# The merge stage of a hybrid decoder block: full products in blocks, or pairs of seven quarter products

## What is computed

```python
proj = rms_norm(h) @ w_in + b_in      # u, v, q, k, vg, r, g_lr, gate_a, gate_b
ya = chunked_sgu(gelu(u), gelu(v), ...)      # 512 x 1024
yb = gla(q, k, vg, gk, r, ...)               # 512 x 1024
merged = sigmoid(gate_a) * (ya @ w_branch_a) + sigmoid(gate_b) * (yb @ w_branch_b)
h = h + merged @ w_out
xn2 = rms_norm(h)
h = h + (silu(xn2 @ w_ffn_gate) * (xn2 @ w_ffn_up)) @ w_ffn_down
y = rms_norm(h)
```

## Time and profile before

| what | value |
|---|---|
| median of three executions | 844.11 us (842.53 to 844.25) |
| the profiled execution | 842.62 us |
| its span, first to last instruction | 840.8 us |
| PE busy | 829.6 us, 99% of the span |
| DVE, ACT, POOL busy | 420.9, 370.9, 342.3 us |
| matmuls of the merge stage | from 266.69 to 441.18 us |
| granted TensorE clock | 0.999 of full speed |

### The profile page before, as it was taken

The page is one execution under the profiler, slowest core; times in us unless marked ns, Lnnn a source line. Parts: engine busy times, 40 slices in busy tenths (PEclk is TensorE's granted clock), DMA queues, the critical chain, the costliest instruction groups (busy, mean ns, idle before and its releaser), DMA issues.

```text
span 840.8 us, 11971 instructions
## 1 busy us (share of the span) xinstructions
PE 829.6 (99%) x4720; PEld 727.9 (87%) x4720; DVE 420.9 (50%) x419; ACT 370.9 (44%) x393; POOL 342.3 (41%) x100
## 2 busy tenths in 40 slices
PE   8999999999999999999999999999999999999996
PEld 7888888788888888888888899999999999888885
DVE  5375337674665721221213269766666667244445
ACT  5522446665666523231312565545445555122233
POOL 4444433324224343434444432644444445544440
PEclk9999999999999999999999999999999999999999
DMA  8842222122112122222225133433333320322212
GB/s 334 287 174 83 86 83 101 51 100 94 49 57 100 51 101 100 100 100 100 98 101 186 65 101 101 128 109 112 109 124 110 106 100 30 138 80 88 93 47 101
DMA packets 17511, 89.88 MB, mean 107 GB/s; under 512 B 1744, under 2 KB 2000, under 8 KB 10704
## 3 DMA queue, kind: packets, MB, share of 16 engines
q1 hardware_dynamic: 15088, 81.83, 27.8%
q10 hardware_dynamic: 2400, 7.73, 2.8%
HBM read 87.46 MB, written 2.10 MB: 107 GB/s over the span
## 4 chain that ended last, share of the span: by engine, by line
PE 88%; DVE 5%; ACT 2%; issue 2%; DMA 2%; POOL 1%; DVEq 0%; SPq 0%; ACTq 0%; POOLq 0%
PE acc L1159 11%; PE acc L1160 11%; PE acc L1161 11%; PE acc L1178 9%; PE acc L1177 9%; PE acc L1176 9%; PE acc L1421 7%; PE acc L1424 7%; PE acc L1423 7%; PE acc L1202 3%; DMA wp<-wstream 1%; DVE vgs L842 1%; PE acc L1295 1%; PE acc L1333 1%; PE acc L1338 1%
## 5 line engine op out<-in xcount | busy, mean ns | idle before, releaser
L333 POOL TENSOR_TENSOR w_lo<-raw,w_hi 128x2048 fp32r<-128x2048 f32 x52 | 239.7, 4610 | 342.9 <-ACT w_hi L410 342.9
L410 ACT ACTIVATE w_hi<-raw 128x2048 fp32r<-128x2048 f32 x52 | 99.3, 1912 | 216.1 <-PE acc L1178 138.8
L1159 PE MATMUL acc<-xt_hi,w_hi 128*128 128x512 f32 (+1 forms) x368 | 140.3, 381 | 0.2 <-ACT yb L520 0.2
L1160 PE MATMUL acc<-xt_lo,w_hi 128*128 128x512 f32 (+1 forms) x368 | 138.1, 375 | 0.0
L1161 PE MATMUL acc<-xt_hi,w_lo 128*128 128x512 f32 (+1 forms) x368 | 138.1, 375 | 0.0
L357 POOL TENSOR_TENSOR A_lo<-wp,A_hi 128x1024 fp32r<-128x1024 f32 x30 | 72.3, 2409 | 97.5 <-ACT A_hi L618 97.5
L1159 PEld LDWEIGHTS acc<-xt_hi,w_hi 128*128 128x128 f32 x368 | 69.3, 188 | 13.9 <-issue 1.1
L1160 PEld LDWEIGHTS acc<-xt_lo,w_hi 128*128 128x128 f32 x368 | 69.3, 188 | 13.1 <-issue 0.9
L1161 PEld LDWEIGHTS acc<-xt_hi,w_lo 128*128 128x128 f32 x368 | 69.3, 188 | 12.4
L1074 DVE TENSOR_TENSOR al<-act,ah 128x1024 fp32r<-128x1024 f32 x11 | 48.2, 4382 | 63.0 <-ACT ah L671 63.0
L1176 PE MATMUL acc<-w_hi,ah 128*128 128x512 f32 x176 | 68.5, 389 | 0.0
(11 more groups left out here) (228 smaller groups left out, 1764.2 us busy)
## 6 DMA issues: line engine op xcount, KB each, us to landing
raw<-wstream SPq DMA_DIRECT2D x52, 1024.0 KB, 4.8
wp<-wstream SPq DMA_DIRECT2D x20, 1024.0 KB, 7.8
h<-x ACTq DMA_DIRECT2D x1, 2048.0 KB, 7.8
xw<-x_t SPq DMA_DIRECT2D x3, 512.0 KB, 9.5
out<-h SPq DMA_DIRECT2D x3, 512.0 KB, 2.6
xn_in<-x SPq DMA_DIRECT2D x2, 512.0 KB, 12.2
xn_in<-x ACTq DMA_DIRECT2D x2, 512.0 KB, 6.6
vbias_bc<-vbias ACTq DMA_DIRECT2D x1, 1024.0 KB, 9.6
```

The source lines that it names most:

```text
L333: pool.tensor_tensor(w_lo[s][:, :], raw[s][:, :], w_hi[s][:, :], ALU.subtract).then_inc(lo_ready, 1)
L410: a.activation(w_hi[s][:, :], raw[s][:, :], ACT.Copy).then_inc(hi_ready, 1)
L1159: pe.matmul(dst, wh[:, k, cs], rh[:, k, ts], start=(k == 0), stop=False)
L1160: pe.matmul(dst, wh[:, k, cs], rl[:, k, ts], start=False, stop=False)
```

## The change

Of the 16 merge blocks the first block of each gate (blocks 20 and 21) stay full products. The other 14 become seven pairs of the feed-forward kind: three pairs of gate blocks (moving operand `xt`), then two pairs with `ya` and two with `yb`. The stage's loops are written out.

- The sums t1 to t4 of `xt` are formed by DVE in the input stage, in the place of `xn_in`, sent by ACT to device memory (`turned_sums`, 4 x 512 KB) between two weight blocks, and brought back by SP before the merge stage.
- For `ya` and `yb` the sums are formed by DVE inside the pairs before (pairs 2, 3 and 4, 5), their high parts are taken by ACT and their low parts by DVE in pairs 3 and 5, and the plain quarters of `ya` and `yb` are written over `xt_hi` (ACT) and `xt_lo` (POOL, `refill`) between the products that still read the old content and those that read the new.
- The joined quarters (`mcq`) of a gate pair get their sigmoid by ACT (`gates_of`, four of 512 elements). Those of a branch pair are multiplied by the gates on POOL (`weighted`, two of 1024 elements). DVE adds the two branches in two halves (`merged_sum`), ACT and DVE split the sums (`merged_high`, `merged_low`).
- The first two output blocks are loaded to another place (`raw_out`), and their low parts are taken by POOL (`low_out`) in pair 7, ahead of `weighted(7)`.

The core of the diff:

```diff
+            v.wait_ge(xw_scaled, KD)
+            v.tensor_tensor(tx[0][:, :, :], x12, x11, ALU.subtract).then_inc(t_formed, 1)
+            v.tensor_tensor(tx[2][:, :, :], x22, x12, ALU.subtract).then_inc(t_formed, 1)
+            v.wait_ge(t_formed, 1)
+            v.tensor_tensor(tx[1][:, :, :], x22, tx[0][:, :, :], ALU.subtract).then_inc(t_formed, 1)
+            v.wait_ge(t_formed, 3)
+            v.tensor_tensor(tx[3][:, :, :], x21, tx[1][:, :, :], ALU.subtract).then_inc(t_formed, 1)
             v.wait_ge(xt_ready, 4)
             values(1)
...
-            for j in range(3):
+            high2(6, 0, block_used, 4)
+            a.wait_ge(t_formed, 4)
+            for n in range(4):
+                a.dma_start(turned_sums[n], tx[n][:, :, :].rearrange("p k t -> p (k t)")).then_inc(t_stored, 16)
+            for j in range(1, 3):
                 high2(6 + j, j % 2, block_used, 3 + j + 1)
...
+            def merge_pair(p):
+                c, nn = (p - 1) % 2, (p + 2) // 2 * 16
+                m = (p - 3) // 2
+                last = p == MERGE_PAIRS
+
+                if p > 1:
+                    form_s2(c)
+                    merge_c12(p - 1)
+                    s_low_of("S2", chain, 7 * p - 2)
+                    v.wait_ge(s_low, 4 * p - 1)
+                    form_s4(c)
+                if p in (4, 6):
+                    t_low_of((p - 4) // 2, 3)
+                if p in (2, 4):
+                    form_t12((p - 2) // 2)
+                if p in (3, 5):
+                    t_low_of(m, 0)
+                merge_u2(p)
+                if p == 1:
+                    merge_u3(p)
+                s_low_of("S4", chain, 7 * p)
+                if not last:
+                    v.wait_ge(s_low, 4 * p)
+                    form_s1(1 - c, nn, p + 1)
+                if p > 1:
+                    merge_u3(p)
+                merge_c22(p)
+                if not last:
+                    form_s3(1 - c)
+                if last:
+                    merged_sum(0)
+                if p in (2, 4):
+                    form_t3((p - 2) // 2)
+                if p in (3, 5):
+                    t_low_of(m, 1)
+                    t_low_of(m, 2)
+                    form_t4(m)
+                merge_c21(p)
+                if not last:
+                    s_low_of("S1", chain, 7 * p + 2)
+                    s_low_of("S3", diff, 7 * p + 3)
+                    v.wait_ge(s_low, 4 * p + 1)
+
+            for p in range(1, MERGE_PAIRS + 1):
+                merge_pair(p)
+            merged_low(0)
+            merge_c12(MERGE_PAIRS)
+            merged_sum(1)
+            merged_low(1)
...
+            def merge_pair(p):
+                c = (p - 1) % 2
+
+                a12_low(c, 7 * p + ((5 if p == 1 else 4) - 7))
+                if p > GATE_PAIRS + 1:
+                    weighted(p - 1)
+                a22_low(c, 7 * p - 1)
+                if p in (4, 6):
+                    refill(3 * ((p - 2) // 2), (ya, yb)[(p - 4) // 2], slice(4, 8), slice(HT, SEQ))
+                if p < MERGE_PAIRS:
+                    a11_low(1 - c, 7 * p + 1)
+                if p in (3, 5):
+                    y = (ya, yb)[(p - 3) // 2]
+                    n = 3 * ((p - 3) // 2)
+                    refill(n + 1, y, slice(0, 4), slice(0, HT))
+                    refill(n + 2, y, slice(4, 8), slice(0, HT))
...
+            pool.wait_ge(product_done, 7 * MERGE_PAIRS - 3)
+            low_out(0)
+            pool.wait_ge(product_done, 7 * MERGE_PAIRS - 2)
+            low_out(1)
+            weighted(MERGE_PAIRS)
...
+                if renewed is not None:
+                    pe.wait_ge(refill_low, 3 * renewed + 1)
+                product("A11", x11, 0, True)
...
+                    pe.wait_ge(joined, 5 * p - 5)
...
+                product("S1", mt1, 2, True)
```

More of the change, by code:

```diff
@@ L296, in _ @@
             sp.wait_ge(lo_ready, B_DOWN)
-            pair_weights(wstream[B_DOWN:B_DOWN + 2], 0)
+            pair_weights(wstream[W_FFN + 2:W_FFN + 4], 0)
             sp.wait_ge(up_done, 2)
[L299 to L304, removed]
+            pair_weights(wstream[W_FFN + 4:W_FFN + 6], 1)
@@ L551, in _ @@
                 a.activation(rs[:, :], bank[2][:, :], ACT.Sqrt, bias=eps).then_inc(osd_ready, 1)
[L554 to L573, removed]
@@ new lines, in a11_high, with a12_high, a22_high, s_high @@
+            def a11_high(c, n):
+                plain_high("A11", c, slice(0, 4), slice(0, P), k1_landed, n)
+            def a12_high(c, n):
+                plain_high("A12", c, slice(4, 8), slice(0, P), k2_landed, n)
+            def a22_high(c, n):
+                plain_high("A22", c, slice(4, 8), slice(P, 2 * P), k2_landed, n)
+            def s_high(name, src, formed):
+                a.wait_ge(s_formed, formed)
+                a.activation(op_hi[name][:, :, :, :], src, ACT.Copy).then_inc(op_high, 1)
@@ new lines, in _, with gates_of @@
+            s_high("S2", chain, 2)
+            s_high("S3", diff, 3)
+            gate_tile(3)
+            a12_high(0, 16)
+            a.activation(xt_hi[:, 0:4, HT:SEQ], mt4[:, :, :], ACT.Copy).then_inc(t_high, 1)
+            def gates_of(p):
+                a.wait_ge(joined, 5 * p)
+                a.wait_ge(taken, 2 * p)
+                if p == GATE_PAIRS:
+                    a.wait_ge(t_formed, 8)
+                for g, (sg, kc) in enumerate(((sg_a, K_GA), (sg_b, K_GB))):
+                    for half in range(2):
+                        t = 2 * p + half
+                        a.activation(sg[:, t, :].rearrange("p (h t) -> p h t", h=2), mcq[:, 2 * half:2 * half + 2, g, :], ACT.Sigmoid,
+                                     bias=par[:, kc + t:kc + t + 1]).then_inc(gates_taken, 1)
@@ new lines, in x_t4_low, with quarters @@
+            def x_t4_low():
+                v.wait_ge(t_high, 4)
+                v.tensor_tensor(xt_lo[:, 0:4, HT:SEQ], mt4[:, :, :], xt_hi[:, 0:4, HT:SEQ], ALU.subtract).then_inc(t_low, 1)
+            form_s1(0, 16, 1)
+            s_low_of("S1", chain, 2)
+            v.wait_ge(s_low, 1)
+            form_s2(0)
+            form_s3(0)
+            s_low_of("S2", chain, 3)
+            v.wait_ge(s_low, 2)
+            form_s4(0)
+            s_low_of("S3", diff, 4)
+            x_t4_low()
+            def quarters(y):
+                return y[:, 0:4, 0:HT], y[:, 0:4, HT:SEQ], y[:, 4:8, 0:HT], y[:, 4:8, HT:SEQ]
@@ L1367, in _ @@
-            pe.wait_ge(tile_free, 4 + 40)
+            for j in range(2):
+                arrived(B_MERGE + j)
+                for t in range(2):
+                    n = 2 * j + t
+                    if n == 2:
+                        pe.wait_ge(osd_ready, HEADS)
+                    if n == 3:
+                        pe.wait_ge(ya_ready, KD)
+                    tile_T(bank[n][:, :], wk(w_hi, j), wk(w_lo, j), t, xt_hi, xt_lo).then_inc(tile_done, 1)
+            x11 = (xt_hi[:, 0:4, 0:HT], xt_lo[:, 0:4, 0:HT])
@@ new lines, in _, with product @@
+            x21 = (xt_hi[:, 4:8, 0:HT], xt_lo[:, 4:8, 0:HT])
+            x22 = (xt_hi[:, 4:8, HT:SEQ], xt_lo[:, 4:8, HT:SEQ])
+            t4 = (xt_hi[:, 0:4, HT:SEQ], xt_lo[:, 0:4, HT:SEQ])
+            def product(name, x, b, start):
+                wh, wl = op_hi[name], op_lo[name]
+                for g in range(2):
+                    dst = bank[b][:, g * HT:(g + 1) * HT]
+                    for k in range(4):
+                        pe.matmul(dst, wh[:, g, k, :], x[0][:, k, :], start=(start and g == 0 and k == 0), stop=False,
+                                  skip_group_check=True)
+                        pe.matmul(dst, wh[:, g, k, :], x[1][:, k, :], start=False, stop=False, skip_group_check=True)
+                        mm = pe.matmul(dst, wl[:, g, k, :], x[0][:, k, :], start=False, stop=(k == 3),
+                                       skip_group_check=True)
+                mm.then_inc(product_done, 1)
```

543 lines of the change are left out of this document (382 added, 161 removed).

## The result

The changed kernel takes **863.60 us** (median of four executions, 861.97 to 864.56), the kernel before 843.32 us in the executions beside it: a ratio of 1.0242, 95% interval 1.0228 to 1.0257. It is 2.4% slower. I had forecast 859 us, 844 to 868. The profiled execution took 862.83 us, with a span of 861.1 us against 840.8 us before.

A forecast was written before the change was run, and what follows sets the result against it. PE, busy 99% of the span, was taken as the bound. Terms -11.2 + 2.7 + 7.1 + 8.1 + 2.0 + 5.3 + 2 = +16.0 us on 842.62 gave 858.6, forecast as 859 us, range 844 to 868.

The forecast's parts named there:

- PE's saving: Merge stage: seven pairs replace stretches of two blocks, each 1.6 us shorter for PE, 11.2 us saved.
- Input stage: Block 7: ACT waits for DVE's four sums, then sends four stores, so PE gets the block 2.7 us late.
- Pairs 3 and 5: DVE's low parts and POOL's refills take turns, so c12 reaches the next pair's S1 late: 7.1 and 8.1 us.
- the better of my two cases: Pair 3: DVE goes first at the port, before POOL's refills, costing 6.0 us; POOL first would cost 8.4.
- u3: Pairs 3, 4 and 5: DVE's added work makes u3 late for PE by 0.2, 1.2 and 0.6 us, 2.0 in all.
- End of the stage: Output projection's first matmul waits for merged_low(0), as merged_sum(0) and it stand behind POOL's low_out: 5.3 us.
- The clock: PE's granted clock falls 4 to 5 us after PE stops; 2 us taken in all for three long gaps.
- My upper bound: Clock term: half of a slow stretch as long as the fall took, 2.4 us, at each of three gaps.
- clock stays low: Rival: the clock stays low after each gap, three times 2.4 us or more, 863 to 872 us; chance 0.09.

The follow-up runs named there:

- run 10: Changed kernel with stores behind block 7, POOL's refills behind t4, reordered stage end, and ACT's high part of t1 ahead of A22's: 833.23 us.
- run 1: Changed kernel, but ACT makes block 7's high part before waiting for the four sums and sending their stores: 857.74 us.
- run 4: Changed kernel, but merged_sum(0), merged_high(0) and merged_low(0) moved earlier in the last pair: 855.17 us.
- run 2: Changed kernel, but in pairs 3 and 5 POOL begins its two refills only when DVE has formed t4: 851.55 us.
- run 3: Changed kernel without POOL's low parts of the first two refills in pairs 3 and 5; POOL only signals: 849.22 us.
- run 9: Kernel before the change, with added SBUF sums nobody waits for, on DVE alone, DVE and POOL together, and POOL alone: 842.64 us, one execution.
- run 8: The kernel of run 10, but in pairs 4 and 6 product A11 does its matmuls with the low part of the renewed operand last: 832.46 us.
- run 5: Kernel before the change, with four added PE waits in its merge stage, made by chains of small DVE instructions: 871.90 us.
- run 7: Changed kernel with the edits of run 1, run 2 and run 4 together, without swapping ACT's high parts of t1 and A22: 838.59 us.

## Why the forecast was right, and where it was off

The sum was +16.0 us, the truth +20.3. The places, the engines and the causes of the gaps were as forecast; the clock term had its mechanism wrong, and was too small by 6.7 us.

- **PE's saving, -11.2.** In run 10 the stage lasts from 266.44 to 431.88, 165.4 us, with waits of 1.5 us: 163.9 us of work against 174.5 before, so -10.6. For the changed kernel 187.2 us less gaps of 18.3 (0.24 of them a wait for u3 in pair 5) and clock of 4.9 give 164.0, or -10.5. Right within 0.7 us; the tally takes run 10's, which does not hang on the clock.
- **Input stage, +2.7.** Measured 3.8. The sums ended at 78.23, where I had 78.8, and PE wanted the block 0.2 us earlier than I had it. The step that was short is the stores: 3.54 us until ACT began block 7, I took 4 x 0.48 from the loads. Runs 1 and 4 show the gap to be apart from the others.
- **Pairs 3 and 5, +7.1 and +8.1.** Measured 5.43 and 7.54. In pair 3 the starts fell together, and the order came out as in the better of my two cases (6.0); in pair 5 POOL was first, as I said. Runs 2, 3 and 9 show the cause: turns at the port.
- **u3, +2.0.** Measured 0.24 in the changed kernel, 0.70 in run 8. My reading is that a late engine catches up while PE stands or is slow, so terms that I had added are not independent; no run isolates it.
- **End of the stage, +5.3.** Measured 5.10, through the chain that I gave; run 4.
- **The clock, +2.** Measured **8.7**. This is the step that failed. I had only the fall after PE's last matmul, 4 to 5 us behind it, and concluded that only the longest gap is surely longer than the fall. In the changed kernel the clock fell at all four gaps, 3.1 to 4.2 us after the last matmul had ended, and at block 7 when PE was back already. Run 5 shows the same: a gap of 3.4 us had its fall too, and PE pays after its return, 1.5 to 1.9 us there, 1.6 to 2.5 us in the changed kernel. My upper bound (2.4 us, three times) was near for one gap; I should have taken it, four times: 9.6. The rival "clock stays low" (863 to 872) had the right mechanism, and the result lies in its range as well as in the upper end of the forecast's; 0.09 was too little for it.

The gaps came out 3.1 us shorter than forecast (22.1 with u3's 0.24, against 25.2), the clock 6.7 us longer, the saving 0.6 us smaller. The range would have held the time without the shorter gaps too (866.7), but that the result lies only 4.6 us from 859 owes something to errors of opposite sign.

What is open: what sets how long PE works slowly after its return. It is not the gap's length alone. Pair 4's gap of 5.43 us stands in three kernels, with 5.4 us of slow work behind it in the changed kernel, 4.9 in run 4 and 3.1 in run 1; in the last the clock fell 5.2 us after the last matmul, in the others 4.0 and 3.5.

## What to carry to other kernels

Where two engines share a port in turns, the price of an instruction is that of the other one's instruction as well. Before you give work to an idle engine, ask what the busy one has to do in those microseconds; here one wait on the idle engine was worth 12 us. Price a gap of a saturated PE at its length and some 2 us more: in these runs every gap of 2.4 us and longer had its slow stretch (1.4 to 2.5 us lost), two of four of 1.9 us, and none of 1.5 us or less. And a change that lightens the bounding engine by 11 us and loses is not a bad change: with the order mended at four places, the same pairs made this kernel 1.1 to 1.3% faster than it was.

## What the runs showed of the hardware

- The granted clock can fall when PE has already begun again (run 5: last matmul at 334.01, the next at 337.80, 0.50 from 338). The same gap of 1.9 us cost 1.5 us at one place and nothing at another (run 7).
- After PE's return the slow pace lasted 3.1 to 5.8 us in all 20 cases of these traces, however long PE had stood (1.9 to 13.3 us). The clock had fallen 2.0 to 5.3 us after the last matmul ahead of the gap.
- The lower clock did not quite double the distance between starts: 0.427 us instead of 0.227 for 512 columns (run 5), 0.213 instead of 0.120 for 256 (changed kernel).
- DVE and POOL took turns instruction by instruction, also where instructions of one engine stood back to back without a semaphore (run 9). The Trainium skill (SBUF — State Buffer, Who interferes with whom) calls the shared port pair an exclusive lock and names a DVE instruction with two SBUF inputs beside a GpSimd one that reads SBUF as a case of it, which these rows bear out.
- Four stores of 512 KB from SBUF to device memory, one behind the other, held ACT's queue for 0.34, 0.46, 0.80 and 1.43 us (changed kernel), loads for 0.45 us each. Why the later stores take longer no run shows.
